# Identity transposes on TensorE ahead of the first turns of projection, mixer and experts

## The chip, the cores and the metric

One core of a Trainium2 chip runs one program. The metric is the device time of one execution in microseconds (us). The engines of the core work beside each other, each through its own order of instructions: TensorE (PE: matrix products; its weight loads are listed apart as PEld), VectorE (DVE), ScalarE (ACT), GpSimd (POOL), and SyncE (SP), which here only issues transfers. They wait for each other by semaphores. TensorE's clock is granted at one of two levels, 1.2 or 2.4 GHz; the profile shows them as 0.50 and 1.00.

## The reference

One encoder layer on two groups of tokens, 1024 ("sample") and 512 ("prompt"), width 1024, float32:

```
proj = rmsnorm(x) @ w_in                     # q, k, v of two kinds of attention
oa   = window attention with sink (+-128 tokens), partial rotary
ob   = 2-D neighbourhood attention (8 x 16) with position bias
x    = x + [rmsnorm(oa) || rmsnorm(ob)] @ w_out
h    = rmsnorm(x)
aff  = softmax(h @ w_router)                 # 16 experts; each takes its best 128 + 64 tokens
ye   = (silu(xe @ w_gate) * (xe @ w_up)) @ w_down * gate
y    = rmsnorm(x + scatter_add(ye))
```

Nothing of what the change adds is part of it.

## The kernel before

Four stages run one after the other, each a block of its own with a barrier between them: `project`, `attend`, `mix` and `experts`. Every stage writes out by hand, for each engine, in which order it does its work, with `wait_ge` and `then_inc` on semaphores; no scheduler moves anything. Products are exact to float32 by splitting each operand into a high part (ScalarE's copy, `hi`) and a low part (VectorE's difference, `lo`) and adding three products (`three_pass`, L124 to L126).

What a "turn" is: TensorE multiplies by the identity to transpose a 128x128 tile into a PSUM bank. All turns need the identity, which each stage loads anew.

`project`: SyncE loads the first x tile, the gain and the identity (L238, L239, semaphore `const_in`). ScalarE sums the squares of a tile, VectorE normalises it into `pj_xn`, TensorE turns it (`turn`, L407: eight transposes into two of the banks `pj_turn`), ScalarE and VectorE split the result. Four tiles make a group, and only then the first product can start. `pj_xn` has one buffer, so VectorE's next tile waits for the turn of the last one. The bank `v_ps` (`pj_v`) is first used much later, by L435.

`attend` is not touched. Its products are L736 (scores) and L772, its turns L745, L753 and L782.

`mix`: for each of 12 tiles of tokens, SyncE loads the attention's result `mx_o`; ScalarE squares it (L924, L941), VectorE makes `mx_merged` in two halves (L1016), TensorE turns it (L1110, eight transposes into banks 0 and 1), ScalarE copies the high part `mx_m_hi` (L962, two copies), VectorE the low part (L1036). For the first tile alone, ScalarE also makes the high parts `mx_w_hi` of the eight rows of weights (L967) behind these copies, and VectorE the low parts `mx_w_lo` (L1042) behind it, before it goes on to `mx_merged` of the second tile. The first tile's products go row by row as `mx_w_lo` comes; with six of the eight rows done, TensorE turns the second tile. Tile by tile the products then follow with no pause. Bank 5 is first written by the products of the second tile. The stage ends with the router's top-k on VectorE, which goes on into the next.

`experts`: VectorE lists the best tokens, TensorE turns the lists (`turn_choice`, L1198), VectorE makes the row numbers of them, GpSimd gathers the first expert's rows (L1372, L1374), TensorE turns these (`turn_x`, L1657 and L1659, banks `ex_turn_ps`), ScalarE and VectorE split them into `ex_xt`. Then a loop of 15 experts and one more expert after it run TensorE's products (L1683, L1685, L1697 to L1701).

Of the kernel before, what the change touches and what calls it, by code (L numbers as in the profile page):

```python
# [28 lines left out]
P = 128  # L29
# [91 lines left out]
def three_pass(nc, out, stationary, moving, first, last):  # L121

    (sh, sl), (mh, ml) = stationary, moving
    nc.tensor.matmul(out, sh, mh, start=first, stop=False)  # L124
    nc.tensor.matmul(out, sh, ml, start=False, stop=False)  # L125
    return nc.tensor.matmul(out, sl, mh, start=False, stop=last)  # L126
# [3 lines left out]

START = 1
REFINE = 6


def inverse_root(dve, step, done, ss, rt, tmp, out, scale):


    mean, sq, corr = tmp
    dve.reciprocal(out, rt).then_inc(step, 1)
    dve.tensor_scalar(mean, ss, scale, EPS, ALU.mult, ALU.add).then_inc(step, 1)  # L140
    dve.wait_ge(step, done + 2)
    dve.tensor_tensor(sq, out, out, ALU.mult).then_inc(step, 1)
    dve.wait_ge(step, done + 3)
    dve.tensor_tensor(corr, sq, mean, ALU.mult).then_inc(step, 1)
    dve.wait_ge(step, done + 4)
    dve.tensor_scalar(sq, corr, -0.5, 1.5, ALU.mult, ALU.add).then_inc(step, 1)
    dve.wait_ge(step, done + 5)
    dve.tensor_tensor(out, out, sq, ALU.mult).then_inc(step, 1)
    dve.wait_ge(step, done + 6)
# [6 lines left out]
def project(nc, d, keep):  # L156
# [4 lines left out]
    with ctx:  # L161
# [11 lines left out]
        ident = sb("pj_ident", [P, P])  # L173
# [10 lines left out]
        turn_ps = [ps(f"pj_turn{i}", [P, 512]) for i in range(4)]  # L184
        out_ps = [ps(f"pj_out{i}", [P, 512]) for i in range(2)]
        v_ps = ps("pj_v", [P, 512])
# [25 lines left out]
        def next_tile(i, after):  # L212

            g, n = divmod(i, CHUNKS)
            if g + 1 < GROUPS and n - after in FIRST_PREP:
                return (g + 1) * G_TILES + FIRST_PREP.index(n - after)
            return None
# [113 lines left out]
        def _(dve):  # L331
# [8 lines left out]
            def norm(t):  # L340
                dve.wait_ge(root, t + 1)
                inverse_root(dve, refined, t * REFINE, ss[:, t:t + 1], rt[:, t:t + 1],
                             [tmp[:, i:i + 1] for i in range(3)], rs[:, t:t + 1], 1.0 / D)
# [53 lines left out]
        @block.tensor  # L397
        def _(pe):
            def turn(t):
                pe.wait_ge(normed, t + 1)  # L400
                for h in range(2):
                    if t >= 2:

                        pe.wait_ge(lo_x, 2 * (t - 2) + h + 1)
                    for j in range(4):
                        c0 = (4 * h + j) * P
                        last = nc.tensor.transpose(turn_ps[2 * (t % 2) + h][:, j * P:(j + 1) * P],  # L407
                                                   xn[:, c0:c0 + P], ident[:])
                    last.then_inc(transposed, 1)

            pe.wait_ge(const_in, 32)
            for t in range(G_TILES):
                turn(t)
            for i in range(N + 1):
                g, n = divmod(i, CHUNKS)
                if i < N:
                    pe.wait_ge(lo_w, i + 1)
                    if i >= 2:
                        pe.wait_ge(taken, i - 1)
                    if n == 0:  # L420
                        pe.wait_ge(lo_x, (g + 1) * (2 * G_TILES))
                    s = i % W_SLOTS
                    for j in range(DT):
                        last = three_pass(nc, out_ps[i % 2][:], (w_hi[:, s, j, :], w_lo[:, s, j, :]),
                                          (x_hi[g][:, j, :], x_lo[g][:, j, :]), j == 0, j == DT - 1)
                    last.then_inc(chunk_done, 1)
                g, q = divmod(i - 1, CHUNKS)
                if q == FIRST_V:

                    pe.wait_ge(taken, i)  # L430
                    if g:
                        pe.wait_ge(v_copied, g)
                    for t in range(G_TILES):
                        c = slice(t * P, (t + 1) * P)
                        last = nc.tensor.transpose(v_ps[:, c], raw[:, ROTATED % 2, c], ident[:])  # L435
                    last.then_inc(v_turned, 1)
                if next_tile(i, 2) is not None:
                    turn(next_tile(i, 2))
# [380 lines left out]
def mix(nc, d, route):  # L819
# [4 lines left out]
    with ctx:  # L824
# [10 lines left out]
        ident = sb("mx_ident", [P, P])  # L835
# [15 lines left out]
        bank = [ps(f"mx_ps{i}", [P, 512]) for i in range(8)]  # L851
# [125 lines left out]
        def _(dve):  # L977
            refines = rounds = 0
            dve.wait_ge(const_in, 32)
            for s in range(-1, TILES + 2):  # L980
# [16 lines left out]
                if 0 <= t < TILES:  # L997
                    dve.wait_ge(root2, t + 1)
                    inverse_root(dve, refined, refines, ss2[:], rt2[:], [tmp2[:, i, :] for i in range(3)],
                                 rs2[:], 1.0 / D)  # L1000
                    refines += REFINE
                    if t >= 2:
# [5 lines left out]
                if t < TILES:  # L1008
                    dve.wait_ge(root1, t + 1)
                    inverse_root(dve, refined, refines, ss1[:], rt1[:], [tmp1[:, i, :] for i in range(3)],  # L1010
                                 rs1[:], 1.0 / HALF)
                    refines += REFINE
                    for k in range(2):
# [31 lines left out]
        @block.tensor  # L1045
        def _(pe):
            pe.wait_ge(const_in, 32)

            def project(t, k, tiles=range(DT)):

                c = slice(k * HALF, (k + 1) * HALF)
                for j in tiles:
                    if t == 0:
                        pe.wait_ge(lo_w, j + 1)
                    last = three_pass(nc, bank[2 + 2 * (t % 2) + k][:], (m_hi[:, t % 2, j, :], m_lo[:, t % 2, j, :]),
                                      (w_hi[:, j, c], w_lo[:, j, c]), j == 0, j == DT - 1)
                return last
# [136 lines left out]
def turn_choice(nc, pe, route, ch, ident):  # L1194

    pe.wait_ge(ch.listed, ch.LISTS)
    for i in range(2):
        last = nc.tensor.transpose(ch.bank[:, i * SEG_ROWS:(i + 1) * SEG_ROWS], route.lists[:, i, :],  # L1198
                                   ident[0:SEG_ROWS, 0:SEG_ROWS])
    last.then_inc(ch.turned, 1)  # L1200
# [21 lines left out]
def experts(nc, d, route):  # L1222
# [6 lines left out]
    with ctx:  # L1229
# [5 lines left out]
        ident = sb("ex_ident", [P, P])  # L1235
# [31 lines left out]
        turn_ps = [ps(f"ex_turn_ps{i}", [P, WIDE]) for i in range(2)]  # L1267
# [263 lines left out]
        def _(dve):  # L1531
# [61 lines left out]
            def add_last(k):  # L1593
# [23 lines left out]
                if k == 0:  # L1617
# [5 lines left out]
                dve.wait_ge(root, len(FIN_ROOTS) + 2)  # L1623
                inverse_root(dve, refined, len(FIN_ROOTS) * REFINE, last_ss[:], last_rt[:],
                             [tmp[:, i, 0:2] for i in range(3)], last_rs[:], 1.0 / D)
# [5 lines left out]
            def finish_norms(c):  # L1631
                if c in FIN_ROOTS:
                    b = FIN_ROOTS.index(c)
                    tiles = slice(b * FIN_BATCH, (b + 1) * FIN_BATCH)
                    dve.wait_ge(root, b + 1)
                    inverse_root(dve, refined, b * REFINE, ss[:, tiles], rt[:, tiles],
                                 [tmp[:, i, :] for i in range(3)], rs[:, tiles], 1.0 / D)
# [13 lines left out]
        def _(pe):  # L1651
# [13 lines left out]
            pe.sem_inc(s_scaled, START)  # L1665
            pe.sem_inc(y_summed, START)
            turn_choice(nc, pe, route, ch, ident)
            pe.wait_ge(gathered_s, 16)
            turn_x(0)
            turn_x(1)  # L1670
# [203 lines left out]
```

## Time and profile before

| | us |
|---|---|
| median of three runs | 2615.8 |
| lowest and highest | 2615.61 and 2617.5 |
| the profiled execution, whole | 2615.77 |
| its span, first to last instruction | 2614.0 |
| TensorE busy, of the span | 2513.8 (96%) |
| VectorE busy | 1711.9 (65%) |
| ScalarE busy | 1477.9 (57%) |
| mean granted TensorE clock | 0.983 |

The profiled execution took as long as the median, so what is worked out in its trace can be set against the median directly; 1.8 us of it lie outside the span. A busy share is a mean over stages: where TensorE has a nine in every slice, it alone matters, and where it has less, the timeline tells who waits for whom. Times in the rows count from the start of the span.

### The profile page before, as it was taken

How to read it: one execution, taken by the hardware profiler on the slowest of the kernel's cores; microseconds unless marked ns; L12 is line 12 of the kernel's file. 1: busy time of each engine (PE TensorE's matmuls, PEld its weight loads, DVE VectorE, ACT ScalarE, POOL GpSimd, SP SyncE). 2: the span in 40 equal slices, each digit the busy share in tenths (PEclk: the TensorE clock that was granted, in tenths of full speed). 3: DMA queues.
4: the chain of work that ended last, by engine and by line, in shares of the span. 5: the costliest groups of instructions: out<-in, count | busy, mean ns of one | idle time of the engine just before them, and what ended most of it. 6: DMA issues, size and time to landing. Idle time of an engine off the chain costs nothing.

```text
span 2614.0 us, 41912 instructions
## 1 busy us (share of the span) xinstructions
PE 2513.8 (96%) x15522; PEld 2228.3 (85%) x15522; DVE 1711.9 (65%) x2658; ACT 1477.9 (57%) x2116; POOL 186.1 (7%) x263
## 2 busy tenths in 40 slices
PE   7999999998985999999999999999999999999997
PEld 5888866656764998989999899998989989899996
DVE  6354267765467766767667676666767667676676
ACT  4333267875654565655656565565555656556574
POOL 0000010100001010110101001010110101101010
PEclk9999999998996999999999999999999999999998
DMA  4333223226436676776767677676776767767685
GB/s 154 122 128 97 65 91 105 98 70 217 140 114 226 226 249 225 250 243 240 247 230 250 227 248 249 225 258 223 255 246 231 248 226 257 239 239 249 225 316 219
DMA packets 95060, 533.61 MB, mean 204 GB/s; under 512 B 10561, under 2 KB 15425, under 8 KB 44801
## 3 DMA queue, kind: packets, MB, share of 16 engines
q1 hardware_dynamic: 87584, 506.58, 54.8%
q0 software_dynamic: 7392, 25.96, 4.5%
q8 instruction: 48, 0.79, 0.1%
q14 instruction: 36, 0.29, 0.0%
HBM read 494.74 MB, written 37.75 MB: 204 GB/s over the span
## 4 chain that ended last, share of the span: by engine, by line
PE 66%; DVE 2%; DMA 1%; ACT 1%; issue 0%; POOL 0%; DVEq 0%; SPq 0%; ACTq 0%; POOLq 0%
PE ex_gate_ps L1683 15%; PE ex_up_ps L1683 15%; PE ex_gate_ps L1685 7%; PE ex_up_ps L1685 7%; PE ex_up_ps L1697 2%; PE ex_down_ps L1697 2%; PE ex_down_ps L1698 2%; PE ex_down_ps L1699 2%; PE ex_down_ps L1700 2%; PE ex_down_ps L1701 2%; PE ex_up_ps L1698 2%; PE ex_up_ps L1700 2%; PE ex_up_ps L1699 2%; PE ex_up_ps L1701 2%; PE ex_turn_ps L1657 1%; PE ex_turn_ps L1659 0%
## 5 line engine op out<-in xcount | busy, mean ns | idle before, releaser
L1534 DVE TENSOR_TENSOR ex_w_lo<-ex_w,ex_w_hi 128x2048 fp32r<-128x2048 f32 x384 | 879.9, 2292 | 461.4 <-ACT ex_w_hi L1451 449.9
L1451 ACT ACTIVATE ex_w_hi<-ex_w 128x2048 fp32r<-128x2048 f32 x384 | 733.4, 1910 | 219.9 <-PE ex_down_ps L1701 107.0
L1683 PE MATMUL ex_gate_ps<-ex_xt,ex_w_hi 128*128 128x384 f32 x2048 | 594.0, 360 | 1.5 <-DVE ex_xt L1540 1.5
L1683 PE MATMUL ex_up_ps<-ex_xt,ex_w_hi 128*128 128x384 f32 x2048 | 592.8, 359 | 0.0
L1685 PE MATMUL ex_gate_ps<-ex_xt,ex_w_lo 128*128 128x192 f32 x2048 | 513.5, 251 | 0.0
L1685 PE MATMUL ex_up_ps<-ex_xt,ex_w_lo 128*128 128x192 f32 x2048 | 512.9, 250 | 0.0
L1685 PEld LDWEIGHTS ex_gate_ps<-ex_xt,ex_w_lo 128*128 128x128 f32 x2048 | 392.0, 191 | 0.6
L1685 PEld LDWEIGHTS ex_up_ps<-ex_xt,ex_w_lo 128*128 128x128 f32 x2048 | 391.2, 191 | 0.0
L1683 PEld LDWEIGHTS ex_gate_ps<-ex_xt,ex_w_hi 128*128 128x128 f32 x2048 | 385.5, 188 | 2.3 <-issue 1.7
L1683 PEld LDWEIGHTS ex_up_ps<-ex_xt,ex_w_hi 128*128 128x128 f32 x2048 | 384.6, 188 | 0.0
L1471 ACT ACTIVATE ex_up_low<-ex_up_ps 128x384 f32<-128x384 f32 x128 | 63.0, 492 | 208.5 <-PE ex_up_ps L1685 208.5
L1469 ACT ACTIVATE ex_gate_low<-ex_gate_ps 128x384 f32<-128x384 f32 x128 | 63.0, 492 | 208.1 <-PE ex_gate_ps L1685 206.7
L335 DVE TENSOR_TENSOR pj_w_lo<-pj_w,pj_w_hi 128x1024 fp32r<-128x1024 f32 x54 | 66.2, 1225 | 157.9 <-ACT pj_w_hi L267 157.9
L634 ACT ACTIVATE at_probs<-at_probs,at_neg_top 128x384 f32<-128x384 f32 (+1 forms) x192 | 109.6, 571 | 32.1 <-DVE at_neg_top L673 17.5
L1392 POOL DMA_INDIRECT acc_scratch<-ex_y_s,ex_scatter_s x15 | 24.2, 1612 | 1434.0 <-DVE ex_y_p L1577 1434.0
L124 PE MATMUL pj_out<-pj_x_hi,pj_w_hi 128*128 128x512 f32 x288 | 113.7, 395 | 1.5 <-DVE pj_x_lo L353 1.5
L125 PE MATMUL pj_out<-pj_x_lo,pj_w_hi 128*128 128x512 f32 x288 | 113.0, 392 | 0.0
L126 PE MATMUL pj_out<-pj_x_hi,pj_w_lo 128*128 128x512 f32 x288 | 113.0, 392 | 0.0
L1561 DVE TENSOR_TENSOR ex_up_sum<-ex_up_ps,ex_up_low 128x384 f32<-128x384 f32 x128 | 71.3, 557 | 51.4 <-ACT ex_up_low L1471 51.3
L1697 PE MATMUL ex_down_ps<-ex_w_hi,ex_ht 128*128 128x512 f32 x256 | 101.4, 396 | 0.0
L1697 PE MATMUL ex_up_ps<-ex_w_hi,ex_ht 128*128 128x512 f32 x256 | 101.3, 396 | 0.0
L1700 PE MATMUL ex_down_ps<-ex_w_hi,ex_ht 128*128 128x512 f32 x256 | 99.8, 390 | 0.0
(242 smaller groups left out, 4122.1 us busy)
## 6 DMA issues: line engine op xcount, KB each, us to landing
ex_w<-in_w_experts SPq DMA_DIRECT2D x384, 1024.0 KB, 4.8
pj_w<-in_w_in SPq DMA_DIRECT2D x54, 512.0 KB, 3.5
at_bias<-in_near_bias SPq DMA_DIRECT2D x8, 1536.0 KB, 8.0
pj_x<-in_x SPq DMA_DIRECT2D x12, 512.0 KB, 4.5
o_scratch<-at_o SPq DMA_DIRECT2D x24, 256.0 KB
mx_o<-o_scratch SPq DMA_DIRECT2D x12, 512.0 KB, 4.2
mx_x<-in_x SPq DMA_DIRECT2D x12, 512.0 KB, 4.3
acc_scratch<-mx_x SPq DMA_DIRECT2D x12, 512.0 KB, 5.1
```

The lines of the kernel that those rows point to most:

```text
L124: nc.tensor.matmul(out, sh, mh, start=first, stop=False)
L125: nc.tensor.matmul(out, sh, ml, start=False, stop=False)
L126: return nc.tensor.matmul(out, sl, mh, start=False, stop=last)
L634: act.activation(p, p, ACT.Exp, bias=neg_top[:, r, h:h + 1], accum_out=sums[:, r, h:h + 1]).then_inc(exped, 1)
L1451: act.activation(w_hi[:, c % SLOTS, :], w[:, c % SLOTS, :], ACT.Copy).then_inc(hi_w, 1)
L1534: dve.tensor_tensor(w_lo[:, c % SLOTS, :], w[:, c % SLOTS, :], w_hi[:, c % SLOTS, :].bitcast(F32), ALU.subtract).then_inc(lo_w, 1)
L1683: nc.tensor.matmul(out[:, b, 0:2 * CAP], w_hi[:, slot, f], xt[:, k, :, :].rearrange("p h c -> p (h c)"), start=k == 0, stop=False)
L1685: last = nc.tensor.matmul(out[:, b, 0:CAP], w_lo[:, slot, f], xt[:, k, 0, :], start=False, stop=k == DT - 1)
L1697: nc.tensor.matmul(out[0], s_hi, hi, start=start, stop=False)
L1698: nc.tensor.matmul(out[0], s_hi, lo, start=False, stop=False)
L1699: nc.tensor.matmul(out[0], s_lo, hi, start=False, stop=stop)
L1700: nc.tensor.matmul(out[1], both, hi, start=start, stop=False)
```

## The change

A helper `keep_running` is added. It issues `n` transposes of the identity, with the identity as the matrix, into the first 128 columns of a PSUM bank that nobody reads before it is written anew. It is called three times, on TensorE: with 20 in `project`, behind the wait for the constants and ahead of the first turn; with 56 in `mix`, behind the wait for the constants; with 30 in `experts`, behind the turn of the lists and ahead of the wait for the gathered rows, once and outside the loop. No semaphore is added, and none is raised by these instructions.

```diff
--- before.py
+++ after.py
@@ -130,6 +130,12 @@
 
 START = 1
 REFINE = 6
+
+
+def keep_running(nc, out, ident, n):
+
+    for _ in range(n):
+        nc.tensor.transpose(out[:, 0:P], ident[:], ident[:])
 
 
 def inverse_root(dve, step, done, ss, rt, tmp, out, scale):
@@ -409,6 +415,7 @@
                     last.then_inc(transposed, 1)
 
             pe.wait_ge(const_in, 32)
+            keep_running(nc, v_ps, ident, 20)
             for t in range(G_TILES):
                 turn(t)
             for i in range(N + 1):
@@ -1045,6 +1052,7 @@
         @block.tensor
         def _(pe):
             pe.wait_ge(const_in, 32)
+            keep_running(nc, bank[5], ident, 56)
 
             def project(t, k, tiles=range(DT)):
 
@@ -1665,6 +1673,7 @@
             pe.sem_inc(s_scaled, START)
             pe.sem_inc(y_summed, START)
             turn_choice(nc, pe, route, ch, ident)
+            keep_running(nc, turn_ps[1], ident, 30)
             pe.wait_ge(gathered_s, 16)
             turn_x(0)
             turn_x(1)
```

In the order built from the two programs, TensorE's rows at the start of the mixer are these before. Names are written<-read; `mx_ps` are the mixer's banks.

```order
L1045 UNCONDITIONAL_BRANCH [waits barrier_Pool_Activation_PE_DVE_SP_release]
L1110 MATMUL mx_ps<-mx_ident,mx_merged 128x128 [waits mx_normed1,mx_const_in]
L1110 MATMUL mx_ps<-mx_ident,mx_merged 128x128 x3
L1110 MATMUL mx_ps<-mx_ident,mx_merged 128x128 [waits mx_normed1]
L1110 MATMUL mx_ps<-mx_ident,mx_merged 128x128 x3
L124 MATMUL mx_ps<-mx_w_hi,mx_m_hi 128x512 [waits mx_lo_w,mx_lo_m]
L125 MATMUL mx_ps<-mx_w_lo,mx_m_hi 128x512
```

And with the change:

```order
L1052 UNCONDITIONAL_BRANCH [waits barrier_Pool_Activation_PE_DVE_SP_release]
L138 MATMUL mx_ps<-mx_ident 128x128 [waits mx_const_in]
L138 MATMUL mx_ps<-mx_ident 128x128 x55
L1118 MATMUL mx_ps<-mx_ident,mx_merged 128x128 [waits mx_normed1]
L1118 MATMUL mx_ps<-mx_ident,mx_merged 128x128 x3
L1118 MATMUL mx_ps<-mx_ident,mx_merged 128x128 [waits mx_normed1]
L1118 MATMUL mx_ps<-mx_ident,mx_merged 128x128 x3
L124 MATMUL mx_ps<-mx_w_hi,mx_m_hi 128x512 [waits mx_lo_w,mx_lo_m]
L125 MATMUL mx_ps<-mx_w_lo,mx_m_hi 128x512
```

The wait for the constants (`mx_const_in`) has moved from the first real turn to the first of 56 added transposes; the real turn keeps its wait for `mx_normed1` and stands behind them.

At the start of the experts TensorE's rows before are the turn of the lists and the turns of the gathered rows.

```order
L1198 MATMUL ex_down_ps<-ex_ident,lists 128x112 [waits ex_const_in,ch_listed]
L1198 MATMUL ex_down_ps<-ex_ident,lists 128x112
L1657 MATMUL ex_turn_ps<-ex_ident,ex_x_s 128x128 [waits ex_gathered_s]
L1657 MATMUL ex_turn_ps<-ex_ident,ex_x_s 128x128 x7
L1659 MATMUL ex_turn_ps<-ex_ident,ex_x_p 128x64 [waits ex_lo_x,ex_gathered_p]
L1659 MATMUL ex_turn_ps<-ex_ident,ex_x_p 128x64 x7
L1736 UNCONDITIONAL_BRANCH
```

And with the change:

```order
L1206 MATMUL ex_down_ps<-ex_ident,lists 128x112 [waits ex_const_in,ch_listed]
L1206 MATMUL ex_down_ps<-ex_ident,lists 128x112
L138 MATMUL ex_turn_ps<-ex_ident 128x128 x30
L1665 MATMUL ex_turn_ps<-ex_ident,ex_x_s 128x128 [waits ex_gathered_s]
L1665 MATMUL ex_turn_ps<-ex_ident,ex_x_s 128x128 x7
L1667 MATMUL ex_turn_ps<-ex_ident,ex_x_p 128x64 [waits ex_lo_x,ex_gathered_p]
L1667 MATMUL ex_turn_ps<-ex_ident,ex_x_p 128x64 x7
L1745 UNCONDITIONAL_BRANCH
```

Thirty transposes without a wait of their own stand between the lists and the gathered rows. No row of another engine moved.

## Rows read from the trace of the kernel before

Columns of a timeline row: start, duration (of all that are merged in it), engine, line, operation, written<-read, shape, count, and in brackets how long the engine was idle before and who ended that. Columns of a stretch: from and to, length, busy us and count of PE, PEld, DVE, ACT and POOL, granted clock, DMA share, GB/s. Columns of a transfer: issued by, count, size, us from issue to landing. Columns of a group: line, engine, operation, names, shape, count, busy us, mean ns of one, idle us before.

**Rows 1.** section 2 of the page: TensorE's busy tenths in 40 slices of 65.35 us
```profile
PE   7999999998985999999999999999999999999997
```

**Rows 2.** projection's opening: timeline, landing of the identity, two stretches
```profile
1.68 0.42 SPq L239 DMA_DIRECT2D pj_ident<-in_ident  x1
...
pj_ident<-in_ident SPq DMA_DIRECT2D x1, 64.0 KB, 4.0
...
10.88 1.94 PE L407 MATMUL pj_turn<-pj_ident,pj_xn 128*128 128x128 f32 x8 [10.88 <-DVE pj_xn L346]
...
26.87 0.76 PE L124 MATMUL pj_out<-pj_x_hi,pj_w_hi 128*128 128x512 f32 x1 [1.50 <-DVE pj_x_lo L353]
...
31.70 0.47 PE L126 MATMUL pj_out<-pj_x_hi,pj_w_lo 128*128 128x512 f32 x1
...
28.20:31.60 3.40, 3.40 (x9) 2.63 (x8) 0.01 (x1) 0.00 (x0) 0.00 (x0) 1.00 0.52 154
...
607.10:611.70 4.60, 4.60 (x21) 3.69 (x20) 4.43 (x10) 1.36 (x5) 0.00 (x0) 1.00 0.70 264
```

**Rows 3.** attention's opening: timeline of TensorE, one stretch, its groups in 335.9-339.1 and 339.1-342.5
```profile
335.99 1.23 PE L736 MATMUL at_score<-k_s,q_s 64*128 64x256 f32 x4 [4.04 <-DMA at_sink<-in_sink]
...
342.00:344.00 2.00, 2.00 (x20) 1.26 (x16) 1.39 (x9) 0.99 (x4) 0.38 (x2) 0.88 0.93 382
...
L736 PE MATMUL at_score<-k_s,q_s 64*128 64x256 f32 x8 | 2.5, 712 | 4.0 <-DMA at_sink<-in_sink 4.0
...
L782 PE MATMUL at_v<-at_ident,at_v_stage 128*128 128x128 f32 x4 | 1.1, 431 | 0.0
...
L736 PE MATMUL at_score<-k_s,q_s 64*128 64x256 f32 x6 | 1.9, 685 | 0.0
...
L745 PE MATMUL at_flip<-at_ident,at_probs 128*128 128x128 f32 x5 | 1.5, 413 | 0.0
...
L782 PE MATMUL at_v<-at_ident,at_v_stage 128*128 128x128 f32 x4 | 1.1, 418 | 0.0
```

**Rows 4.** mixer's opening: timeline, landing of the identity, the stretch with the rise
```profile
589.04 0.42 SPq L888 DMA_DIRECT2D mx_ident<-in_ident  x1
...
mx_ident<-in_ident SPq DMA_DIRECT2D x1, 64.0 KB, 4.7
...
596.63 1.94 PE L1110 MATMUL mx_ps<-mx_ident,mx_merged 128*128 128x128 f32 x8 [13.29 <-DVE mx_merged L1016]
...
599.10 7.73 ACT L967 ACTIVATE mx_w_hi<-mx_w 128x1024 fp32r<-128x1024 f32 x8
...
601.55 0.76 PE L124 MATMUL mx_ps<-mx_w_hi,mx_m_hi 128*128 128x512 f32 x1 [2.98 <-DVE mx_w_lo L1042]
...
604.00:606.00 2.00, 2.00 (x8) 1.58 (x7) 2.00 (x3) 2.00 (x3) 0.00 (x0) 0.68 1.02 408
...
610.32 1.42 DVE L1016 SCALAR_TENSOR_TENSOR mx_merged<-mx_o,mx_rs,mx_gain_out 128x512 f32<-128x512 f32 x2
...
611.75 1.03 PE L1110 MATMUL mx_ps<-mx_ident,mx_merged 128*128 128x128 f32 x8
```

**Rows 5.** timeline of TensorE about two idle times in the mixer, one stretch
```profile
759.78 0.50 PE L124 MATMUL mx_ps<-mx_w_hi,mx_m_hi 128*128 128x512 f32 x1 [2.58 <-DVE mx_m_lo L1036]
...
772.86 0.29 PE L1131 MATMUL mx_ps<-mx_gather_parts,mx_parts 128*128 128x16 f32 x2
...
774.00:776.00 2.00, 0.00 (x0) 0.00 (x0) 0.52 (x2) 1.51 (x3) 0.00 (x0) 0.99 0.36 147
```

**Rows 6.** experts' opening: timeline of TensorE, the stretch with the rise
```profile
807.76 0.64 PE L1198 MATMUL ex_down_ps<-ex_ident,lists 112*128 112x112 f32 x2 [17.96 <-DVE lists L1161]
...
815.14 1.97 PE L1657 MATMUL ex_turn_ps<-ex_ident,ex_x_s 128*128 128x128 f32 x8 [6.74 <-DMA ex_x_s<-h_scratch,index]
...
820.34 0.68 PE L1683 MATMUL ex_gate_ps<-ex_xt,ex_w_hi 128*128 128x384 f32 x1 [1.50 <-DVE ex_xt L1540]
...
822.00:824.00 2.00, 2.00 (x11) 2.00 (x9) 2.00 (x2) 0.70 (x1) 1.69 (x2) 0.56 0.28 41
```

## The prediction

> **What bounds the kernel now.** Read the forty slices of the page first: TensorE stands at nine tenths or more nearly everywhere [rows 1]. The dips are the first slice (the projection's opening), the tenth (the mixer's), the twelfth and thirteenth (the mixer's end and the experts' opening) and the last. Outside them TensorE sets the pace, and what an opening gains or loses is carried unchanged to the end. Next come the openings themselves, in the timeline, and the granted clock by stretches. The clock has two levels, 1.2 and 2.4 GHz (0.50 and 1.00 in the clock column); in 3.40 us from 28.2 on 8 weights of 128x512 products were loaded, 0.43 us a product at the low one; in 4.60 us from 607.1 on 20, 0.23 a product, at the high one [rows 2]. The clock column reads 1.00 in both, so before the first rise it is not to be trusted and the products tell the level.
>
> Four times the clock rose, and each time the reader should look at how long TensorE had worked without a break before. Projection: from 26.87 until the record at 31.70 (0.47 us, no longer 0.63), 4.9 us [rows 2]. Attention: from 335.99; the stretch from 342 to 344 has a mean of 0.88, so 0.48 us of it was low and the rise was at 342.5, 6.5 us [rows 3]. Mixer: from 601.55; mean 0.68 in 604 to 606, rise at 605.3, 3.75 us [rows 4]. Experts: from 820.34; mean 0.56 in 822 to 824, rise at 823.8, 3.4 us [rows 6]. The mean of the four is 4.65 us, the ends are 3.4 and 6.5. The whole cold time that lies in front of products in the three openings is 4.9 + 3.75 + 3.4 = 12 us, and with 0.43 instead of 0.23 us for a product about 0.45 of it is loss, so even a perfect warm-up could give back no more than 12 x 0.45 = 5.4 us, 0.2% of the run.
>
> **What one added turn costs.** The nearest rows are the same instruction, a 128x128 f32 transpose: eight in 1.94 us at the low clock, the last record 0.42 long, (1.94 - 0.42) / 7 = 0.215 us each; eight in 1.03 at the high clock, (1.03 - 0.27) / 7 = 0.11 each [rows 4]. They stand in TensorE's own order ahead of the stage's first real turn, so the question at each place is whether they are through when that turn's data are ready.
>
> **Projection, 20 turns.** They wait for the identity, which is issued at 1.68 and lands 4.0 us later, at 5.7. 20 x 0.215 = 4.3, through at 10.0; the real turn waits for VectorE until 10.88 [rows 2]. Hidden, with 0.8 us to spare. Can the clock rise inside? They give 4.3 us of unbroken work; two of the four rises needed less. Then tile 0's turn (eight) is 0.9 us shorter, but TensorE works only in bursts of eight transposes (1.94 us) between there and 26.87, and at the high clock half of that, so the products at 26.87 start low again. Term: -0.1 (0 to -0.9). If the identity landed 0.8 us later, the cover would be gone and each further tenth would be paid in full.
>
> **Mixer, 56 turns.** This is the place that decides. The identity is issued at 589.04 and lands 4.7 us later, 593.75 [rows 4]. The real turn of tile 0 was ready at 596.63, only 2.9 us later, room for 13 turns. With the rise after 4.65 us: 22 turns low, 34 high, 34 x 0.11 = 3.7, through at 593.8 + 4.65 + 3.7 = 602.2. With a rise at 3.4 us it is 601.6, at 6.5 us 603.1. The tile-0 turn is thus 5.6 us late (5.0 to 6.5). Queued behind it: ScalarE's two copies mx_m_hi, behind these its eight copies mx_w_hi (from 599.10), VectorE's eight mx_w_lo, TensorE's products (from 601.55), and VectorE's mx_merged of tile 1 (610.32) for the second turn at 611.75 [rows 4]. Nothing there waits for the loads any more, so the lateness moves through all. Some comes back: the turn itself is at the high clock: the last of eight ends 1.03 after the first instead of 1.94. Of these 0.9 us I give back 0.8, since the two copies then follow each other without a pause; mx_w_hi is 5.6 - 0.8 = 4.8 us late. The products then start at 606.35, with TensorE idle since 603.2. An idle time of 2.58 us was survived at the high clock; after 773.15 the clock was low at 776.0, 2.8 us later [rows 5]. Here 3.1 us are idle, so I take it that the clock falls and the products start low once more, for 4.65 us instead of 3.75: 0.9 x 0.45 = +0.4. And if it does stay high? 3.75 x 0.45 = 1.7 us of products are saved, but the second turn waits for both halves of mx_merged, which ended at 611.74 (610.32 + 1.42), and it ran from 611.75 with the second half wanted half a microsecond later; it can come forward by 0.4 at most. Term: 4.8 + 0.4 = +5.2 (4.0 to 6.5).
>
> **Experts, 30 turns.** They stand behind the two turns of the lists (from 807.76, 0.64 long) and ahead of the turn that waits for the gathered rows until 815.14 [rows 6]. 30 x 0.215 = 6.45, from 808.2 to 814.7, or 813.9 with a rise: hidden, 0.4 us to spare. If the clock is up at 815.14, the copies and turns that lie between there and the products at 820.34 shrink by half of the first eight transposes (0.5 us) and by half of the second turn, eight smaller ones (0.45): products at 819.4. But from 814 to 819.4 TensorE works only some 1.5 us, which I take for too little to hold the clock (no row shows it), so the products start low again, for 4.65 us against the 3.4 of this trace: +1.25 x 0.45 = +0.55. Term: -0.95 + 0.55 = -0.4 (-2.5 if the clock stays up throughout, +1.4 if neither happens and the rise comes late).
>
> **Attention.** Not changed, but this trace's 6.5 us before the rise is the longest; a usual 4.65 gives back part of 1.9 x 0.45, since TensorE shares the pace there. Term: -0.4 (-0.8 to 0).
>
> **Sum.** -0.1 + 5.2 - 0.4 - 0.4 = +4.3 us on the profiled execution's 2615.77, which is also the median (2615.8): 2620.1, I say 2620.0, 0.16% slower. A measurement of this kernel can tell about 0.2%, 5.2 us, from no change; so the forecast is "no change", near the edge.
>
> **A rule against it.** The added turns raise the clock only if turns count as work for the gate. The trace: from 335.9 to 339.1 TensorE ran 8 score products (2.5 us) and 4 turns (1.1 us), and the clock stayed low; from 339.1 to 342.5 it ran 6 products (1.9 us) and 9 turns (1.5 and 1.1 us), and the clock rose [rows 3]. The stretch with more turns and fewer products is the one that ends in the rise. The Trainium skill says the contrary ("TensorE: Matmul & The Clock Gate", Part 4: PE-mode transpose): transposes do not count as busy in the same way, and the full clock does not engage for them. By the trace the mixer's term is +5.2, by the rule it is the first rival below.
>
> **Rivals.**
> 1. Turns do not raise the clock; all added ones run low. What it does: 56 x 0.215 = 12.0, through at 605.8, 9.1 us late with nothing given back; +0.4 for the later rise of the products; projection and experts stay hidden (10.0 and 814.7), the latter with +0.55; attention -0.4. 9.1 + 0.4 + 0.55 - 0.4 = +9.7: 2625.4, slower by 0.37%. It decides as soon as the 56 turns keep their low-clock step. For: in no row did turns alone go before a rise, and the projection's bursts of eight, from 10.88 on, raised nothing. Against: rows 3. This is the case on the other side of the forecast.
> 2. The mechanism of the forecast, but sizes at their bad ends: rise at 6.5 us in the mixer (+6.5), nothing gained in the experts: +5.5 to +7, 2621.3 to 2622.8, slower.
> 3. The clock, once up, stays up in the openings, and the mixer's delay is partly covered. Mixer: 4.0; experts: -2.5; projection: products at 26.87 high too, 4.9 x 0.45 = -2.2. Sum -0.7 to -1.1: 2615, the same. A true gain needs the mixer's turn not to be late, for instance an identity that lands much sooner than 593.75; then -5 or so, 2611. Nothing in the rows speaks for it.
> 4. The turns are not there at all (their result has no reader): 2615.8. The order printed from the built program shows them in place, so no chance worth a number.
>
> **How the numbers follow.** The forecast's case 58% (2617.3 to 2621.0), rival 2 17%, rival 1 18%, rival 3 7%, of which 3% are a gain of over 5.2 us. Slower by over 0.2%: 0.17 + 0.18 = 0.35; faster by over 0.2%: 0.03; within: 0.62. The range leaves out some 6% below 2617.0 and 4% above 2626.0, for rival 1 with a late rise.
>
> **What would show it.** Of the added turns, the first record of each group at 5.7, 593.8 and 808.2. In the mixer the step between them must fall from 0.215 to 0.11 after 3.4 to 6.5 us, the last one must start near 602, tile 0's turn right behind without idle time, mx_w_hi near 604, the first products near 606.3 with 0.43 us each, the second turn near 617. If the step stays at 0.215, rival 1 holds. In the projection the first real turn must still be at 10.88, in the experts at 815.14 plus the mixer's lateness, 820.3. The forecast is wrong if the mixer's first turn is not late, or if the time between it and the end of the mixer shrinks, which would mean that a slack absorbs it.

## The result: 0.14% slower, and the profile after

| | median us | lowest to highest | runs |
|---|---|---|---|
| before | 2615.52 | 2614.17 to 2619.21 | 22 |
| after | 2619.54 | 2617.87 to 2621.73 | 22 |

The ratio is 1.0014, with a 95% interval of 1.0008 to 1.0020: slower, by 4.0 us between the medians, which is clear of 1 and smaller than the 0.2% that was called distinguishable. In the later runs one execution of e7 (3050 us) and one of the kernel before beside it (2752 us) ran at a granted clock of 0.75 and 0.84 and are left out of the ratios. The forecast was 2620.0. The profiled execution took 2618.58 us (span 2616.8), 2.8 us more than that of before.

First the places of the change. The first piece below is the timeline of TensorE of the kernel after (start, duration, engine, line, operation, written<-read, shape, count, idle time before and who ended it), the second shows stretches of it (from and to, length, busy time of PE, PEld, DVE, ACT and POOL, granted clock, DMA share, GB/s). L138 is the line of the added turns.

```profile
6.13 4.01 PE L138 MATMUL pj_v<-pj_ident 128*128 128x128 f32 x20 [6.13 <-DMA pj_ident<-in_ident]
11.16 1.09 PE L413 MATMUL pj_turn<-pj_ident,pj_xn 128*128 128x128 f32 x8 [1.02 <-DVE pj_xn L352]
13.70 1.09 PE L413 MATMUL pj_turn<-pj_ident,pj_xn 128*128 128x128 f32 x8 [1.45 <-DVE pj_xn L352]
19.28 1.94 PE L413 MATMUL pj_turn<-pj_ident,pj_xn 128*128 128x128 f32 x8 [4.48 <-DVE pj_x_lo L359]
...
27.27 0.77 PE L124 MATMUL pj_out<-pj_x_hi,pj_w_hi 128*128 128x512 f32 x1 [1.50 <-DVE pj_x_lo L359]
...
593.19 7.96 PE L138 MATMUL mx_ps<-mx_ident 128*128 128x128 f32 x56 [10.34 <-DMA mx_ident<-in_ident]
600.99 1.04 PE L1118 MATMUL mx_ps<-mx_ident,mx_merged 128*128 128x128 f32 x8
605.05 0.47 PE L124 MATMUL mx_ps<-mx_w_hi,mx_m_hi 128*128 128x512 f32 x1 [3.03 <-DVE mx_w_lo L1049]
605.36 0.40 PE L125 MATMUL mx_ps<-mx_w_lo,mx_m_hi 128*128 128x512 f32 x1
...
812.62 0.64 PE L1206 MATMUL ex_down_ps<-ex_ident,lists 112*128 112x112 f32 x2 [17.97 <-DVE lists L1169]
813.05 6.07 PE L138 MATMUL ex_turn_ps<-ex_ident 128*128 128x128 f32 x30
820.16 1.09 PE L1665 MATMUL ex_turn_ps<-ex_ident,ex_x_s 128*128 128x128 f32 x8 [1.03 <-DMA ex_x_s<-h_scratch,index]
822.32 0.68 PE L1667 MATMUL ex_turn_ps<-ex_ident,ex_x_p 64*128 64x64 f32 x8 [1.07 <-DVE ex_xt L1548]
824.50 0.44 PE L1692 MATMUL ex_gate_ps<-ex_xt,ex_w_hi 128*128 128x384 f32 x1 [1.50 <-DVE ex_xt L1548]
...
825.55 0.57 PE L1692 MATMUL ex_gate_ps<-ex_xt,ex_w_hi 128*128 128x384 f32 x1
```
```profile
16.50:19.00 2.50, 0.00 (x0) 0.00 (x0) 2.36 (x6) 2.50 (x4) 0.00 (x0) 0.50 1.03 365
596.00:598.00 2.00, 2.00 (x18) 2.00 (x17) 0.67 (x2) 0.00 (x0) 0.00 (x0) 0.86 1.03 414
601.90:605.00 3.10, 0.12 (x2) 0.00 (x0) 2.61 (x4) 3.10 (x5) 0.00 (x0) 1.00 1.04 416
764.00:766.00 2.00, 2.00 (x6) 1.57 (x5) 0.30 (x2) 1.73 (x3) 0.00 (x0) 0.50 0.48 195
818.00:820.00 2.00, 1.13 (x8) 0.89 (x6) 0.06 (x1) 0.00 (x0) 0.83 (x1) 0.89 0.82 260
```

What to see there:

- **Mixer.** The 56 turns start at 593.19, with the identity, and the real turn of tile 0 stands right behind them, with no idle time, at 600.99; it was at 596.63 [rows 4]. The mean clock of 0.86 in 596 to 598 means 0.56 us at 0.50, so the clock rose at 596.56: nothing but added turns had run since 593.19, for 3.4 us. The pause of 3.03 us that follows is left at the high clock: the products at 605.05 take 0.47 and then 0.23 us each, from start to start.
- **Projection.** The 20 turns take 4.01 us, less than the 4.5 of twenty at the low clock, and the next eight turns take 1.09 us instead of 1.94 [rows 2]: the clock is up. By 16.5 it is down again (0.50), during the 4.48 us in which TensorE has nothing to do, and the products at 27.27 start low as they did before.
- **Experts.** The 30 turns lie between the lists' turns and the gathered rows, 820.16, and TensorE still waits 1.03 us: hidden. The clock rises at 818.44, holds to the first products at 824.50, and is lost at 825.3: the record of a 128x384 product is 0.36 us long at the high clock and 0.57 at 825.55.

To see where the time went, the same instruction of each stage is taken in both traces, and its start in the one is subtracted from the start in the other:

| place | before | after | difference | of this stretch |
|---|---|---|---|---|
| last product of the projection | 331.56 | 332.50 | +0.94 | +0.94 |
| end of attention | | | -0.48 | -1.42 |
| mixer, turn of tile 0 | 596.62 | 600.98 | +4.36 | |
| mixer, turn of tile 2 | 626.91 | 630.07 | +3.16 | +3.64 |
| last products of the mixer | 772.07 | 776.91 | +4.84 | +1.68 |
| first product of the experts | 820.34 | 824.50 | +4.16 | -0.68 |
| turn of the second expert's rows | 909.88 | 912.65 | +2.77 | -1.39 |
| end | 2613.96 | 2616.80 | +2.84 | +0.07 |

The +3.64 is the mixer's opening. The +1.68 after it is in one place. Of the kernel after, TensorE's timeline:

```profile
760.23 0.29 PE L1139 MATMUL mx_ps<-mx_gather_parts,mx_parts 128*128 128x16 f32 x2
763.08 0.50 PE L124 MATMUL mx_ps<-mx_w_hi,mx_m_hi 128*128 128x512 f32 x1 [2.56 <-DVE mx_m_lo L1043]
...
763.92 0.63 PE L124 MATMUL mx_ps<-mx_w_hi,mx_m_hi 128*128 128x512 f32 x1
764.35 0.63 PE L125 MATMUL mx_ps<-mx_w_lo,mx_m_hi 128*128 128x512 f32 x1
```

It is the idle time of [rows 5], 2.56 us here and 2.58 before. Before, the clock was kept through it; here it fell at 763.8, 0.7 us behind its end, and the products run at 0.43 us for 3.4 us, which costs 3.4 x 0.45 = 1.5. The attention's -1.42 is the reverse: low for 3.4 us (337.2 to 340.6), where [rows 3] had 6.5. Neither stands near an added turn. The fall at 763.8 may belong to the change all the same: the runs below show it once more, in e1. The -1.39 of the first expert is taken up below too.

### The profile page after: what moved, and what is told of

The parts are those of the page before. It is cut to its first block, busy times and chain, and to the rows that moved or that the text cites. A ratio compares the mean times of both kernels' runs of the same rounds, so it can differ in the third digit from the quotient of the medians.

```text
span 2616.8 us, 42122 instructions
## 1 busy us (share of the span) xinstructions
PE 2525.8 (97%) x15628; PEld 2240.5 (86%) x15628; DVE 1711.8 (65%) x2658; ACT 1477.0 (56%) x2116; POOL 182.7 (7%) x263
## 4 chain that ended last, share of the span: by engine, by line
PE 66%; DVE 2%; DMA 1%; ACT 1%; issue 0%; POOL 0%; DVEq 0%; SPq 0%; ACTq 0%; POOLq 0%
PE ex_gate_ps L1692 15%; PE ex_up_ps L1692 15%; PE ex_gate_ps L1694 7%; PE ex_up_ps L1694 7%; PE ex_up_ps L1706 2%; PE ex_down_ps L1706 2%; PE ex_down_ps L1708 2%; PE ex_down_ps L1707 2%; PE ex_down_ps L1709 2%; PE ex_down_ps L1710 2%; PE ex_up_ps L1707 2%; PE ex_up_ps L1709 2%; PE ex_up_ps L1708 2%; PE ex_up_ps L1710 2%; PE ex_turn_ps L1665 1%; PE ex_turn_ps L1667 0%
## 5 line engine op out<-in xcount | busy, mean ns | idle before, releaser
L1706 PE MATMUL ex_down_ps<-ex_w_hi,ex_ht 128*128 128x512 f32 x256 | 101.4, 396 | 0.0
L1707 PE MATMUL ex_down_ps<-ex_w_lo,ex_ht 128*128 128x512 f32 x256 | 99.8, 390 | 0.0
```

Source lines behind the costliest of these rows:

```text
L1706: nc.tensor.matmul(out[0], s_hi, hi, start=start, stop=False)
L1707: nc.tensor.matmul(out[0], s_hi, lo, start=False, stop=False)
```

## Experiments

In all of them but e3 and e4 the edit is told against the kernel before, with the function of the change (keep_running) added where turns are; in e3 and e4 it is told against the kernel after. The kernel before, run beside them, had medians of 2615.2 to 2615.3. Where two traces are compared stage by stage, a start is set against the start of the stage, which is the end of the stage ahead of it. The added turns write banks that nobody reads, so the output is untouched.

**1. The mixer's 56 alone** (e1), and **the others without it** (e2).

```
 keep_running(nc, bank[5], ident, 56)        # e1: this call only
```
```
 keep_running(nc, v_ps, ident, 20)           # e2: these two only
...
 keep_running(nc, turn_ps[1], ident, 30)
```

> Only the 56 turns of the mixer are left; those of projection and experts are taken out. Theory A (all of the loss is the late first turn of the mixer, and the other two places give back under 1 us): +4.0 to +5.0 us against before, 2620, slightly slower than the change itself by the 0.5 to 0.9 that the experts gained. Theory B (a part of the loss comes from projection or experts, whose first products came 0.4 us later and whose clock fell anew): +3 or less.

> The 20 turns of the projection and the 30 of the experts stay, the 56 of the mixer go. Theory A: -0.5 to -1 us against before, 2614.8; in the trace the experts' first product stands about 4.3 us behind their first real turn instead of 5.2. Theory B: above before by 1 us or more.

e1: 2621.65 us (2618.89 to 2623.31), ratio 1.0018, 1.0009 to 1.0027. e2: 2614.58 (2613.23 to 2615.18), ratio 0.9993, 0.9984 to 1.0002, with the experts' first product 4.33 us behind their first real turn. The loss comes with the mixer's 56 turns and with no other part of the change; at +6.4 us between the medians e1 lies above the 4 to 5 that were expected. In e1's timeline of TensorE

```profile
592.77 8.55 PE L138 MATMUL mx_ps<-mx_ident 128*128 128x128 f32 x56 [10.16 <-DMA mx_ident<-in_ident]
601.16 1.04 PE L1117 MATMUL mx_ps<-mx_ident,mx_merged 128*128 128x128 f32 x8
605.23 0.47 PE L124 MATMUL mx_ps<-mx_w_hi,mx_m_hi 128*128 128x512 f32 x1 [3.03 <-DVE mx_w_lo L1048]
605.53 0.40 PE L125 MATMUL mx_ps<-mx_w_lo,mx_m_hi 128*128 128x512 f32 x1
```

the turns take 8.55 us (the rise came later), and the pause of 3.03 us is again left at the high clock. Against the start of the stage the turn of tile 2 is 4.06 us late. A further 1.6 us comes at the end of the stage, as in the kernel after: behind the idle time that ends at 763.14 (2.58 us here) the clock was low from 764.6 to 768.0. Stretches of e1, and of e4 (112 turns, taken up next), in which the same idle time of 2.58 us ended at 769.14:

```profile
766.00:768.00 2.00, 2.00 (x6) 1.59 (x5) 0.76 (x6) 1.97 (x3) 0.00 (x0) 0.50 0.20 80
```
```profile
769.00:774.00 5.00, 4.86 (x21) 3.95 (x22) 2.12 (x10) 3.64 (x5) 0.00 (x0) 1.00 0.27 108
```

All fourteen traces of this case have this idle time, 2.55 to 2.59 us long. The clock was lost behind it in two, after and e1, which are the two kernels with 56 turns; e4 kept it. Whether that is chance or goes with the 56 turns stays open, since neither of the two kernels was traced twice. If it goes with them, some 1.6 us of their loss is made there and not in the opening.

**2. How many turns.** 13, as many as the prediction found room for (e3), and 112 (e4), both with the 20 and the 30 in place.

```
-keep_running(nc, bank[5], ident, 56)
+keep_running(nc, bank[5], ident, 13)        # e3;  112 in e4
```

> The mixer gets 13 turns, as many as fit between the landing of the identity and the data of the first real turn at the low clock (13 x 0.215 = 2.8 us of 2.9). Theory A: the first real turn is not late (within 0.2 us), the clock rises a little earlier than before; since the second turn waits for VectorE, the mixer gains at most 0.4 to 0.7 us: total -0.5 to -1.5 against before. Theory B (any added turns in the mixer cost something beyond the late first turn): above before.

> The mixer gets 112 turns, twice as many. Theory A: the added 56 all run at the high clock, 56 x 0.11 = 6.1 us, and every one of them is carried to the end: +10.1 us against before, 2625.6. Theory of rival 1 (turns do not raise or hold the clock): 56 x 0.215 = 12 us more, +16. If part of the lateness is absorbed by a slack: under +8.

e3: 2614.02 (2612.18 to 2615.29), ratio 0.9992, 0.9983 to 1.0001. e4: 2624.61 (2623.01 to 2625.47), ratio 1.0034, 1.0021 to 1.0048. In e4's trace the first real turn and the turn of tile 2 are both 6.6 us later against the start of the stage than in the kernel after: 56 more turns at the high clock, 56 x 0.11 = 6.2 (6.1 by their mean step of 0.109), and 0.5 because the clock rose 4.4 us behind the first turn instead of 3.4. From 56 to 112 the median grows by 5.1 us; 6.6 less the 1.6 at the end of the mixer, which e4 doesn't have, would be 5.0, but the interval of e4, five runs, is too wide to lean on that. So every turn beyond those that fit the wait for mx_merged is paid in full, and 13 cost nothing that can be measured. TensorE's timeline and a stretch, e3 and then e4:

```profile
595.35 3.04 PE L138 MATMUL mx_ps<-mx_ident 128*128 128x128 f32 x13 [11.73 <-DMA mx_ident<-in_ident]
598.18 1.40 PE L1118 MATMUL mx_ps<-mx_ident,mx_merged 128*128 128x128 f32 x8
602.61 0.77 PE L124 MATMUL mx_ps<-mx_w_hi,mx_m_hi 128*128 128x512 f32 x1 [3.03 <-DVE mx_w_lo L1049]
...
599.50:602.00 2.50, 0.07 (x1) 0.00 (x0) 2.05 (x3) 2.50 (x4) 0.00 (x0) 1.00 1.02 411
602.00:606.00 4.00, 3.39 (x9) 2.70 (x10) 4.00 (x5) 3.93 (x6) 0.00 (x0) 0.57 1.03 411
```
```profile
607.15 1.04 PE L1118 MATMUL mx_ps<-mx_ident,mx_merged 128*128 128x128 f32 x8
611.22 0.77 PE L124 MATMUL mx_ps<-mx_w_hi,mx_m_hi 128*128 128x512 f32 x1 [3.03 <-DVE mx_w_lo L1049]
...
610.00:612.00 2.00, 0.78 (x2) 0.71 (x3) 2.00 (x2) 2.00 (x3) 0.00 (x0) 0.70 0.02 8
```

Here the same pause, 3.03 us, ends with the clock at the low level, in both: the first product's record is 0.77 long, and the clock fell at 602.3 in e3 (1.00 until 602.0, then a mean of 0.57) and at 610.8 in e4. In the kernel after and in e1 it held. Four traces of four kernels, one length of pause, two outcomes. The row of e3 also shows how thin the cover of 13 is: the identity landed at 595.35 in that execution, and tile 0 was 1.3 us late.

**3. The experts' opening** (e6: the 30 turns alone; e7: 8 instead of 30).

```
 turn_choice(nc, pe, route, ch, ident)
+keep_running(nc, turn_ps[1], ident, 30)     # e6;  8 in e7
 pe.wait_ge(gathered_s, 16)
```

> Only the experts' 30 turns are left. In the four traces with them the first expert's chunk of 32 products takes 4.55 us, in the two without them 4.64 us, over the whole expert 1.4 us. If the 30 turns do it: 4.55 here, and with the 0.9 us by which the products come earlier 2613.0 (-2.3). If it came from elsewhere (the projection's turns, chance): 4.64 and 2614.4.

> Only 8 turns in the experts, 1.7 us at the low clock and over 6 us before the gathered rows are there, so the clock cannot be high at the products. If the short step of the first expert needs products that start at the high clock: 4.64 us a chunk and the same time as before, 2615.3. If it only needs some turns ahead of the products: 4.55 and 2614.

e6: 2614.17 (2612.57 to 2616.17), ratio 0.9997, 0.9988 to 1.0006. e7: 2615.84 (2613.81 to 2618.24 but for the one execution of 3050), ratio 1.0001, 0.9992 to 1.0011. Neither can be told from no change. The two were made to settle the -1.39 of the first expert. There the products run without a break at the full clock and yet have two steps: 32 of them (16 of each width) take 4.64 us in the trace of before and 4.55 in that of after, over the 70 us of this expert; all later experts have 4.55 in every trace. e2, e3 and e4, which all have the 30 turns, had 4.55, and e1, without them, had 4.64, so I held the 30 turns for the cause. e6 has the 30 turns and 4.64: that fell. Then the projection's 20 were left, and e9 was to show it.

**4. The projection's 20 alone** (e9).

```
 pe.wait_ge(const_in, 32)
+keep_running(nc, v_ps, ident, 20)
 for t in range(G_TILES):
```

> Only the projection's 20 turns. All five traces with these 20 turns show the short step in the first expert (4.55 us a chunk of 32 products), all five without them the long one (4.64). If the turns of the projection do it, however far away: 4.55 here and 2613.9 (-1.4). If it falls by chance from execution to execution: either step, and a time near before, 2615.3.

2617.09 (2616.0 to 2618.11), ratio 1.0006, 0.9997 to 1.0015, the step 4.55: the step that was expected if the 20 turns make it, and not the 2613.9 that went with it. The pair that follows takes this apart as well: the kernels of e6 and of e2 once more, unchanged.

> The kernel of e6_experts_30 once more, for its trace alone. If the step of the first expert is fixed by the program: 4.64 us a chunk again. If by chance: 4.55 is as likely.

> The kernel of e2_no_mixer once more, for its trace alone. If the step of the first expert is fixed by the program: 4.55 us a chunk again. If by chance: 4.64 is as likely.

Times of 2613.58 and 2615.86 us. Stretches of 50 us in the first expert, in this order: before, after, e6, its repetition e11, e2, its repetition e12.

```profile
835.00:885.00 50.00, 50.00 (x347) 50.00 (x346) 36.33 (x40) 29.58 (x33) 0.00 (x0) 1.00 0.65 233
```
```profile
835.00:885.00 50.00, 50.00 (x354) 50.00 (x353) 36.92 (x39) 29.78 (x34) 0.00 (x0) 1.00 0.71 257
```
```profile
835.00:885.00 50.00, 50.00 (x346) 50.00 (x346) 36.33 (x40) 29.74 (x33) 0.00 (x0) 1.00 0.65 233
```
```profile
835.00:885.00 50.00, 50.00 (x354) 50.00 (x353) 36.81 (x40) 29.75 (x33) 0.00 (x0) 1.00 0.67 240
```
```profile
835.00:885.00 50.00, 50.00 (x354) 50.00 (x353) 36.81 (x40) 29.75 (x33) 0.00 (x0) 1.00 0.68 240
```
```profile
835.00:885.00 50.00, 50.00 (x347) 50.00 (x346) 36.33 (x39) 29.68 (x33) 0.00 (x0) 1.00 0.66 235
```

TensorE is busy throughout, at a clock of 1.00, with 354 products or with 346 or 347, and one and the same kernel shows the one in one execution and the other in the next, in both pairs. So the program alone does not set the step; what does stays open. The -1.39 in the comparison of the two traces can't be put down to the change. Nor is every tie to it excluded: of the eight traces with the projection's 20 turns seven have 4.55 (e12 has not), of the six without them one (e11).

**5. Turns behind the real turn** (e8), where nothing waits for them.

```
                         last.then_inc(turned1, 1)
+                    if t == 0:
+                        keep_running(nc, bank[5], ident, 20)
```

> Only 20 turns in the mixer, put behind its first real turn and ahead of the first product, in the 3 us in which TensorE waits for the weights' low parts: 1.9 us of real turns and then 20 x 0.215 = 4.3 at the low clock, 2.6 to 4.3 with a rise inside. Theory A (what is lost is the lateness of what stands behind): the first real turn is at 596.6 as before, the first product at 601.6 to 602.9, up to 1.3 us late but then mostly at the high clock, and the second turn, which waits for VectorE until 611.1, within 0.7 us of before: no difference that can be measured, 2615 +- 1. If it is the number of added turns that costs, wherever they stand: +2.

2616.27 (2612.79 to 2618.86), ratio 1.0003, 0.9994 to 1.0013. TensorE's timeline:

```profile
596.03 1.94 PE L1116 MATMUL mx_ps<-mx_ident,mx_merged 128*128 128x128 f32 x8 [13.34 <-DVE mx_merged L1022]
597.76 3.85 PE L138 MATMUL mx_ps<-mx_ident 128*128 128x128 f32 x20
601.36 0.48 PE L124 MATMUL mx_ps<-mx_w_hi,mx_m_hi 128*128 128x512 f32 x1
```

The warm-up does what it is for: the products start high (0.48, against 0.76 in [rows 4]), and without delay. It still gives next to nothing, since the second turn is at 610.52, 1.23 us earlier than before, of which 0.64 is the stage's own earlier start: the 0.6 us that is left is what the chain over VectorE's mx_merged lets through, and by the turn of tile 2 only 0.3 of it are left. The time that the products saved becomes idle time. Bank 5 takes these 20 turns as it took the 56, so it is not the bank that costs.

**6. All pauses filled** (e5), and the projection's part of it alone (e10). Turns are put ahead of the first real turn only as far as the wait for it covers them, and then into every pause up to the products. The core of e5:

```
+keep_running(nc, v_ps, ident, 20)
-for t in range(G_TILES):
+for t, fill in enumerate((8, 20, 20, 10)):
     turn(t)
+    keep_running(nc, v_ps, ident, fill)
...
+keep_running(nc, bank[5], ident, 13)        # mixer, ahead
+keep_running(nc, bank[5], ident, 24)        # mixer, behind tile 0
...
+keep_running(nc, turn_ps[1], ident, 30)     # experts, ahead
 turn_x(0), turn_x(1)
+keep_running(nc, down_ps[1], ident, 8)
 turn_x(2)
+keep_running(nc, down_ps[1], ident, 12)
```

> All openings are filled without being made late: projection 20 turns ahead and 8, 20, 20 and 10 behind its four real turns, mixer 13 ahead and 24 behind its first real turn, experts 30 ahead, 8 between and 12 behind the turns of the gathered rows. If the added turns hold the clock as real work does, all three stages' products start at the high clock: projection -4.9 x 0.45 = -2.2 us, experts -3.4 x 0.45 - 0.9 = -2.4 (and -1.4 more if the step of the first expert's products is the short one), mixer -0.5: 2609 to 2611. If turns only raise the clock but don't hold it, it is e3_mixer_13 again, 2614.

> Only the projection's turns of e5_filled: 20 ahead of and 8, 20, 20 and 10 behind its four real turns. Measures the projection's part of the gain alone. In the trace of e5_filled the projection's last product was 2.7 us earlier than before and the products ran high from the first on. Expected -2.7, 2612.6, with the short step in the first expert -4.0, 2611.3. If the gain of e5_filled came from the experts alone: 2615.

e5: **2608.33 us (2607.54 to 2611.22), ratio 0.9977, 0.9968 to 0.9986**, 6.9 us under the kernel before and 11.2 under the one after; every run of it is below every run of either, and the median is somewhat below the 2609 to 2611 that were expected. e10: 2612.95 (2611.32 to 2617.47), ratio 0.9992, 0.9983 to 1.0001, so by its times alone the projection's part is not clear of no change; its trace has the last product of the projection 2.30 us earlier, and the short step in the first expert. TensorE's timeline in e5, and one stretch:

```profile
5.88 4.53 PE L138 MATMUL pj_v<-pj_ident 128*128 128x128 f32 x20 [5.88 <-DMA pj_ident<-in_ident]
10.95 1.18 PE L413 MATMUL pj_turn<-pj_ident,pj_xn 128*128 128x128 f32 x8 [0.54 <-DVE pj_xn L352]
11.97 1.04 PE L138 MATMUL pj_v<-pj_ident 128*128 128x128 f32 x8
...
18.94 1.16 PE L413 MATMUL pj_turn<-pj_ident,pj_xn 128*128 128x128 f32 x8 [2.08 <-DVE pj_x_lo L359]
...
26.47 0.47 PE L124 MATMUL pj_out<-pj_x_hi,pj_w_hi 128*128 128x512 f32 x1 [0.73 <-DVE pj_x_lo L359]
...
593.59 1.66 PE L1119 MATMUL mx_ps<-mx_ident,mx_merged 128*128 128x128 f32 x8
595.09 2.78 PE L138 MATMUL mx_ps<-mx_ident 128*128 128x128 f32 x24
598.24 0.47 PE L124 MATMUL mx_ps<-mx_w_hi,mx_m_hi 128*128 128x512 f32 x1 [0.36 <-DVE mx_w_lo L1050]
...
811.60 1.09 PE L1668 MATMUL ex_turn_ps<-ex_ident,ex_x_s 128*128 128x128 f32 x8 [0.95 <-DMA ex_x_s<-h_scratch,index]
812.52 1.04 PE L138 MATMUL ex_down_ps<-ex_ident 128*128 128x128 f32 x8
...
815.93 0.43 PE L1697 MATMUL ex_gate_ps<-ex_xt,ex_w_hi 128*128 128x384 f32 x1
...
12.00:26.00 14.00, 9.88 (x84) 8.75 (x81) 12.19 (x25) 8.60 (x16) 0.00 (x0) 1.00 0.76 261
```

The longest pause that is left in the projection is 2.08 us, and the clock stays up from 11.2 to the end of the stage (332.0), where the kernel after had lost it by 16.5. Against the trace of before, the last product of the projection is 2.73 us earlier, the mixer's turn of tile 2 3.65, its last product 3.57, the experts' first product 4.42, the second expert's rows 7.42 and the end 6.70. The projection and the experts bring the gain (of the experts' 3.1, some 1.4 may be the step of the first expert), the mixer nearly none, as in e8. The experts' pauses were not filled in a run of their own.

## Why the forecast held, step by step

The forecast was right in sign and size, and in the main in its cause: no difference to speak of, on the slow side, and the loss made in the mixer by turns that outlast the wait. The experiments bear out the cause: without the 56 no loss (e2), with 13 none (e3), alone the whole (e1), and with 112 a further 5 to 6.6 us (e4). Not foreseen was the second piece of the mixer's loss, the 1.7 us behind the late idle time. By its own steps:

- **Do turns raise the clock?** Yes, and alone. In the mixer only added turns ran in the 3.4 us before the rise. The reading of [rows 3] was right, rival 1 (+9.7, all at the low step) is out, and so is, for this chip and these 128x128 f32 transposes, the rule of the Trainium skill ("TensorE: Matmul & The Clock Gate", Part 4: PE-mode transpose) that the full clock does not engage for transposes: 56 of them took 7.96 us, not 12.0.
- **The prices.** 0.215 and 0.11 us a turn were taken from the eight-turn rows. They held: e4's 112 turns take 14.56 us, and 4.4 / 0.215 = 20 of them low and 92 x 0.11 = 10.1 high make 14.5.
- **Projection, -0.1.** Hidden, as said: 20 turns through before the real turn, which came at 11.16 instead of 10.88, because VectorE's pj_xn was 0.3 us later in that trace (10.95 in e5, with the same 20). The clock was lost again before the products, as said. The stage came out +0.94, because the products were low for 6.1 us instead of 5.0. It is the single execution rather than the turns: in the five other traces with these 20 turns and no more (e2, e3, e4, e9, e12) the stage's last product lies between 0.60 us early and 0.30 late against before, in the five without any (e1, e6, e7, e8, e11) between 0.39 early and 0.26 late.
- **Mixer, +5.2: for the opening, which it priced, too high: 3.6 in this trace and 4.1 in e1.** Three steps of it were off in this trace. The rise came after 3.4 us, not 4.65, so that the 56 took 7.8 us and not 8.4, and the first turn was 4.8 us late, not 5.6 (600.98 against 596.62, less the -0.48 with which the stage began). mx_w_hi was then 4.0 late, not 4.8. And I let the clock fall in the pause of 3.1 us, with +0.4 for it, where it held in this trace. In e1 the rise came after 4.6 us, as assumed, and the clock held too. What follows then is the branch that the prediction had beside it: the products save 1.7 us, and the second turn comes forward only by what VectorE allows. The row behind that, of the kernel after:

```profile
614.63 1.32 PE L1118 MATMUL mx_ps<-mx_ident,mx_merged 128*128 128x128 f32 x8 [0.91 <-DVE mx_merged L1023]
```

  TensorE, which had no idle time there in [rows 4], waits 0.91 us for mx_merged, and the stage is 3.4 us late at this turn and 3.6 at the next. With the clock falling (e3, e4) this wait is not there. The 4.0 was the lower end of the term, and the measured 3.6 lies below it. Two of the signs that were named did not come: the first products were to start near 606.3 at 0.43 us each (605.05, at 0.23), and the second turn near 617 (614.63). A third, that the time from the mixer's first turn to its end must not shrink, was met only by the fall at 763.8: by tile 2 that time had shrunk by 1.2 us (+4.36 to +3.16), and the 1.68 made it up. With it the mixer as a whole lost 5.3 us in this trace and 5.6 in e1, close to the +5.2 for a reason that the term does not hold.
- **Experts, -0.4.** The turns were hidden and the first product came 0.7 us earlier against its stage (0.95 said; 0.7 to 0.9 in all eight traces with the 30 turns). Then it ran low again, as said, though later than I thought: the clock was still up at the first products and fell at 825.3.
- **Attention, -0.4.** Here -1.42, by the same 3.4 us of low clock instead of 6.5. It is a matter of the single execution, and the reading behind the term was off: before is no outlier here. In all twelve other traces the clock was low for 6.8 us at this place (335.64 to 342.46 in before), and the stage came out 0 to 0.44 us shorter.
- **The bound on a perfect warm-up, 5.4 us, was too low.** It counted only the low-clock time of products. e5 gained 6.7 us in its trace (6.9 between the medians; the interval, 3.7 to 8.4, holds 5.4 as well). Left out were the turns themselves, which are shorter at the high clock and bring the first product 0.4 us forward in the projection and 0.8 in the experts, and the step of the first expert, 1.4 us.
- **What was missing** is that these sizes differ from trace to trace where nothing was changed: how long the products run low before a rise (in the experts' opening without turns 3.1 us in e10 and 6.3 in e9), the step of the first expert (1.4 us), and the time from the last expert's turn to the end, which is 1.4 us longer in e12 than in before and 0.1 in e2, the same kernel as e12. To these comes the pause of 2.6 us in the mixer (1.5 us), for which chance is not shown. In the two profiled executions the pause (+1.7) and the step (-1.4) nearly cancel, and the attention's -1.42 brings their difference, 2.8, below that of the medians, 4.0. That the sum of 4.3 met the latter within 0.3 us is partly luck: the mixer's opening was priced 1.1 to 1.6 us too high, and a loss of about that size that was not in the sum came at the mixer's end.

## What to carry to other kernels

Work that only keeps the engine running may stand ahead of a stage's first real instruction only for as long as that instruction waits anyway; count it from the landing of what it reads, not from the end of the last work, and each piece beyond it is paid in full on an engine that sets the pace. Raising the clock is no gain in itself: it must still be up when the long run of products starts, so the filling belongs in every pause between the rise and there (e5, 2608.3 us). One block ahead gives little even where it is short enough (e3, 2614.0), and costs where it is too long (after, 2619.5). Where another engine's chain sets the pace behind the opening, as VectorE's mx_merged in the mixer, even a perfect warm-up gives next to nothing.

## What the runs showed of the hardware

- 128x128 f32 transposes alone take the clock from 1.2 to 2.4 GHz, after 3.4 us in the mixer of the kernel after, 4.4 in e4 and 4.6 in e1, and then take 0.11 instead of 0.215 us each.
- The length of a pause does not settle its outcome. One of 3.03 us kept the clock twice (after, e1) and lost it twice (e3, e4); one of 2.55 to 2.59 us late in the mixer kept it in twelve traces and lost it in two (after, e1). In e5's openings no pause between groups of turns was above 2.08 us, and none lost it. In the 4.48 us of the projection it was lost, and in the experts at 825.3, after the products had begun.
- At a granted clock of 1.00 and with TensorE busy all the time, the same program ran 354 or 347 of the first expert's products in 50 us, by the execution. No cause was found; it decides 1.4 us here, and a comparison of single traces has to allow for it.
